# Final stage of a hybrid-mixer and expert layer: residual rows before expert rows, whole adds on VectorE

## The reference

```
h = h + hybrid_mixer(rms_norm(h, mix_norm_w), ...)
xn = rms_norm(h, ffn_norm_w)
h = h + hierarchical_moe(xn, ...)      # two expert rows a token
out = rms_norm(h, final_norm_w)[:, N_META:]
```

## Time and profile before

| | us |
|---|---|
| median of 3 timed runs | 1332.23 |
| lowest, highest | 1330.84, 1334.21 |
| the profiled execution | 1330.3 |
| its span in the trace | 1328.4 |

### The profile page before, as it was taken

How to read it: one execution, slowest core, us unless ns; L and a number is a source line. 1 busy time by engine, 2 the same in 40 slices (tenths; PEclk the granted TensorE clock), 3 DMA queues, 4 the chain that set the end, 5 groups by cost and what they waited for, 6 DMA issues and landing times.

```text
span 1328.4 us, 19059 instructions
## 1 busy us (share of the span) xinstructions
PE 1289.4 (97%) x7544; PEld 1128.8 (85%) x7544; DVE 902.2 (68%) x1060; ACT 722.6 (54%) x919; POOL 178.5 (13%) x144
## 2 busy tenths in 40 slices
PE   6999999999999999999998999999999999999987
PEld 5989999999999999967887788888888888888864
DVE  6654545455545464634247998898898898988867
ACT  6351235123612351423214887888887888888744
POOL 0020112011201120420001011111111111111000
PEclk9999999999999999999996999999999999999999
DMA  7100010001000000306534999999999999999978
GB/s 208 49 16 33 17 33 33 32 18 33 33 19 31 33 33 1 128 7 262 165 145 169 341 387 370 387 380 386 408 393 382 391 386 375 392 384 390 370 276 345
DMA packets 38047, 273.56 MB, mean 206 GB/s; under 512 B 8147, under 2 KB 8403, under 8 KB 25700
## 3 DMA queue, kind: packets, MB, share of 16 engines
q1 hardware_dynamic: 28340, 251.67, 49.9%
q0 software_dynamic: 9216, 16.80, 3.3%
q10 hardware_dynamic: 432, 4.27, 0.8%
HBM read 260.11 MB, written 29.36 MB: 218 GB/s over the span
## 4 chain that ended last, share of the span: by engine, by line
PE 85%; DVE 6%; DMA 4%; ACT 3%; issue 1%; SPq 0%; DVEq 0%; POOLq 0%; ACTq 0%
PE bank L590 11%; PE bank L592 11%; PE bank L591 11%; PE bank L1290 8%; PE bank L1292 8%; PE bank L1291 8%; PE bank L1417 4%; PE bank L1415 3%; DMA w_raw<-in_w_up 3%; PE bank L477 2%; PE bank L481 2%; PE bank L479 2%; PE bank L581 2%; DVE w_lo L955 1%; DVE arena L1820 1%; PE bank L1406 1%
## 5 line engine op out<-in xcount | busy, mean ns | idle before, releaser
L955 DVE TENSOR_TENSOR w_lo<-w_raw,w_hi 128x2048 fp32r<-128x2048 f32 x192 | 432.9, 2286 | 35.2 <-ACT w_hi L736 34.8
L736 ACT ACTIVATE w_hi<-w_raw 128x2048 fp32r<-128x2048 f32 x192 | 360.6, 1915 | 82.3 <-DMA w_raw<-in_w_up 52.4
L1290 PE MATMUL bank<-xn_hi,p_hi 128*128 128x364 f32 (+1 forms) x672 | 229.0, 341 | 2.1 <-DVE p_lo L1755 2.1
L1292 PE MATMUL bank<-xn_hi,p_lo 128*128 128x364 f32 (+1 forms) x672 | 216.5, 322 | 0.0
L1291 PE MATMUL bank<-xn_lo,p_hi 128*128 128x364 f32 (+1 forms) x672 | 216.0, 321 | 0.0
L590 PE MATMUL bank<-w_hi,xgT_hi 128*128 128x512 f32 x512 | 206.3, 403 | 2.9 <-DVE xgT_lo L1013 2.9
L592 PE MATMUL bank<-w_hi,xgT_lo 128*128 128x512 f32 x512 | 201.2, 393 | 0.0
L591 PE MATMUL bank<-w_lo,xgT_hi 128*128 128x512 f32 x512 | 200.7, 392 | 0.0
L1290 PEld LDWEIGHTS bank<-xn_hi,p_hi 128*128 128x128 f32 x672 | 127.5, 190 | 2.9 <-DVE p_lo L1755 2.5
L1291 PEld LDWEIGHTS bank<-xn_lo,p_hi 128*128 128x128 f32 x672 | 127.7, 190 | 0.3
L1292 PEld LDWEIGHTS bank<-xn_hi,p_lo 128*128 128x128 f32 x672 | 127.1, 189 | 0.0
(11 more groups left out here) (253 smaller groups left out, 2032.5 us busy)
## 6 DMA issues: line engine op xcount, KB each, us to landing
w_raw<-in_w_down SPq DMA_DIRECT2D x32, 2048.0 KB, 10.3
w_raw<-in_w_gate SPq DMA_DIRECT2D x31, 2048.0 KB, 10.9
w_raw<-in_w_up SPq DMA_DIRECT2D x31, 2048.0 KB, 9.8
p_raw<-in_w_tiles SPq DMA_DIRECT2D x28, 512.0 KB, 3.3
arena<-y_rows SPq DMA_DIRECT2D x8, 1024.0 KB, 14.2
arena<-in_tokens SPq DMA_DIRECT2D x10, 416.0 KB
w_out_raw<-in_w_out SPq DMA_DIRECT2D x4, 1024.0 KB, 7.9
arena<-in_tokens SPq DMA_DIRECT2D x8, 512.0 KB, 4.3
```

Of the source, the lines that this page charges most:

```text
L736: nc.scalar.activation(w_hi[m][:, half], wraw[m][:, half], ACT.Copy).then_inc(hi_done[m], 1)
L955: nc.vector.tensor_tensor(w_lo[m][:, half], wraw[m][:, half], w_hi[m][:, half].bitcast(F32), ALU.subtract).then_inc(lo_done[m], 1)
L1290: nc.tensor.matmul(out[:, 0:n], p_hi[slot][:, k, :], hi, start=(k == 0), stop=False)
L1292: m = nc.tensor.matmul(out[:, 0:n], p_lo[slot][:, k, :], hi, start=False, stop=(k == KD - 1))
```

## The change

SyncE loads all eight tiles of residual rows before it waits for `moe_done`; before, it loaded tiles 4 to 7 between the expert rows. VectorE adds the whole first expert row (1024 columns) to the residual, where it added 512 columns. TensorE has two identity products a tile in place of three. The order of the functions on each engine stays, and no semaphore or buffer is new.

```diff
-            for t in range(4):
+            for t in range(FT):
                 residual_rows(t)
             sp.wait_ge(moe_done, 1)
             for t in range(FT):
                 if t == 4:
                     sp.wait_ge(u_done, E)
                 sp.dma_start(yf[t].rearrange("p (k d) -> p k d", k=2), ...)
-                if 2 <= t < 6:
-                    residual_rows(t + 2)
...
                 nc.tensor.matmul(pair_of[0], ident, yf[t][:, D:D + 512], start=True, stop=False)
                 nc.tensor.matmul(pair_of[1], ident, yf[t][:, D + 512:2 * D], start=True, stop=False)
-                nc.tensor.matmul(pair_of[1], ident, yf[t][:, 512:D], start=False, stop=False)
...
-            def first_half(t):
+            def first_row(t):
                 dve.wait_ge(hf_loaded[t], 48 if t + NXS < NC else 32)
                 dve.wait_ge(yf_loaded[t], 16)
-                tt(hf[t][:, 0:512], hf[t][:, 0:512], yf[t][:, 0:512], ALU.add).then_inc(f_sum, 1)
+                tt(hf[t], hf[t], yf[t][:, 0:D], ALU.add).then_inc(f_sum, 1)
...
-            first_half(0)
-            first_half(1)
+            first_row(0)
+            first_row(1)
...
-            first_half(2)
+            first_row(2)
             for t in range(FT):
                 from_psum(t)
                 if t:
                     scaled(t - 1)
                 if t + 3 < FT:
-                    first_half(t + 3)
+                    first_row(t + 3)
             scaled(FT - 1)
```

## The result

The changed kernel is slower. Its median is 1336.8 us (10 runs, 1334.81 to 1342.0) against 1331.38 for the kernel before in runs beside it (10 runs, 1329.52 to 1338.02). The ratio is 1.0039, 95% interval 1.0024 to 1.0054, that is 5.2 us (3.2 to 7.2). The forecast of no change that can be measured, +0.9 us at 1333.1 us, was wrong, and the time lies 0.6 us above the range (1330.0 to 1336.2).

The account below looks back on a forecast made before the run. TensorE bounded the last stage at 3.50 us a tile; VectorE would take over at 3.53. A delay of 2.2 us less 1.3 gave +0.9 on the median of 1332.2, so 1333.1 us, range 1330.0 to 1336.2.

Parts of the forecast that it names:

- x: Delay of expert 30's scatter and everything behind GpSimd's memset, put at 2.2 us; the end moves by x - 1.3.
- The extra wait of 4.8 us: Extra hold of an earlier scatter behind weight packets, scaled by packet size to 1.3 us for the last scatter.
- The turn-taking: Scatter and residual packets alternating on the DMA engines once the scatter starts; 1.4 us, of which 0.9 was counted.
- TensorE doesn't hold it up: Last stage: TensorE waits about 1 us for expert 31's low half, then at 2.64 us a tile stays ahead of VectorE.
- the clock as a rival: TensorE pauses before its first last-stage tile and drops to 1.2 GHz: +16 us, 1348; chance 0.02.
- the bound moved from TensorE to VectorE: Last stage: VectorE needs 3.53 us a tile, TensorE 2.64, so the period stays near the earlier 3.50.
- the 6.9 us of TensorE's products: Gain from one identity product fewer a tile, 8 x 0.86 us, if TensorE alone bounded the last stage; chance 0.04.
- The neutral point: Start of VectorE's third whole add at which the change neither gains nor loses: 1298.6, against 1297.11 before.
- the scatter waits for the drained queue: Rival: expert 30's scatter is held until the residual rows are drained, x from 4.2 to 5.4, 1335.7 us; chance 0.18.

Follow-up runs that it names:

- e3: Changed kernel with the two low-half instructions of expert 31 ahead of VectorE's second whole add; ratio to the kernel before 1.0019.
- e1: Changed kernel with residual tiles 4 to 7 loaded between the expert rows again, so only the compute part is new; ratio to the kernel before 1.0005.
- e6: Changed kernel with residual tiles 4 to 7 issued only once the last scatter has landed, still ahead of the expert rows; ratio to the kernel before 1.0014.
- e7: Changed kernel with loads in the old order, low half of expert 31 first, SyncE waiting for the scatters itself; ratio to the kernel before 0.9983.
- e8: As e7, but tiles 5 to 7 go back to half adds and three identity products; ratio to the kernel before 0.9982.
- e9: Kernel before with one edit: SyncE waits for the scatters itself instead of for GpSimd's memset; ratio to the kernel before 0.9993.
- e4: As e1, but 2 MB of unused weights, in packets four times as large, load where the changed kernel loads residual tiles 4 to 7; one run, 1337.87 us.
- e2: Kernel before with only the new load order, keeping half adds and three identity products; ratio to the kernel before 1.0043.
- e5: Changed kernel with only residual tiles 4 and 5 ahead of the memset, tiles 6 and 7 between the expert rows; ratio to the kernel before 1.0009.

## Why the prediction was wrong

The step that failed is the size of x: "The extra wait of 4.8 us, shrunk by 4/14.6, is 1.3 us." I had a row of a scatter held under load, and scaled its hold with the size of the packets, without a row that showed such a law. The runs show that there is none over these ranges: with packets of 4 KB, with packets four times as large, and with 1.88 to 2.95 MB to move, the first packet is at 4.1 to 4.3 us. Against the 1.5 of before that is an extra wait of 2.7, where I had 1.3. The turn-taking behind it was mis-sized too: from the first packet to the landing the scatter took 3.1 us in place of 1.6, 1.5 more, where I counted 0.9. So x is 4.3, not 2.2. That is 2.1 of the 3.6 us by which the trace missed.

The row I scaled was also a poor one to scale: its issue took 2.20 us, that of the last scatter 0.97. The scatter of 1208.26 in the same trace has an issue of 1.07 and a first packet at 4.2, behind weight packets; taken as it is, it would have given the extra wait of 2.7.

The other 1.5 us is a step that I worked out for an undelayed stage and didn't work out again with x: "TensorE doesn't hold it up". Behind the late memset the second whole add waits until 1298.85, the low half of expert 31 is queued behind it on VectorE, and TensorE waits 4.63 us where I wrote about 1. The second rows also came 3.87 us after the first and not 2.57. Then came the lower clock and a second tile of 4.0 us. e3 moves the two instructions and takes 1.6 us away. I had the clock as a rival for the whole stage, at +16 us; it was low for one tile.

Right, by the same steps: the bound moved from TensorE to VectorE (3.53 us a tile forecast and measured, whole adds 1.22 to 1.23 long and stepping by 1.13), so the 6.9 us of TensorE's products were worth nothing by themselves (e1). The neutral point held too. It was put at 17.96 us after the scatter's issue (1298.6 - 1280.64) for the third add; the measured 20.69, with the 0.2 that the fourth add waits and the 1.47, gives 4.4 for the measured 4.45.

The rival "the scatter waits for the drained queue" named the place and, with x from 4.2 to 5.4 and 1335.7 us, nearly the time. That it came near is luck, since its reason is not what happened: the scatter started with 2.4 us of loads still to come. I gave it 0.18 since the packets are 3.6 times smaller. All loaded scatters in the earlier trace rows spoke for it, with a median of 11.8 us against 3.1, and one mechanism of my own making spoke against it.

## What to carry to other kernels

A load that is moved ahead of a wait fills a gap in the transfers, but ask whose transfer used that gap. Here it was the scatter that everything behind the wait depends on; 2 MB saved from the busy stretch cost 4.3 us at its start. When a transfer's delay under load has to be guessed, look through the loaded rows for one like it in all else, its issue time above all, and take that delay as it is; a scaling law needs rows of its own. And once a start is late, go through each engine's queue again: the instruction that waits for it blocks what stands behind it, here two short instructions that TensorE needed.

## What the runs showed that was not expected

- A scatter issued by GpSimd while SyncE's queue has much to move (1.88 to 2.95 MB) moved its first packet 4.1 to 4.3 us after its issue in six kernels, with 4 KB packets and with 16 KB packets, and 1.5 us after it where the queue had 0.07 to 0.58 MB to move (before, e6, e7, e8, e9). What makes up the 4.2 us is open: a fixed amount of bytes ahead (some 1.3 MB, 0.41 MB/us in the 3.2 us that follow the 0.97 of the issue; 1.4 MB in e4) and a fixed time, each cut short when the queue runs dry, fit these runs about equally well. A fixed number of packets doesn't.
- TensorE's clock during expert 31's last product was not the same from kernel to kernel, though the idle time ahead of it was. It was low in part of it in the changed kernel, e1, e2, e5 and e7, and not in the seven other traces. The changed kernel shows it low from 1288 on, the kernel before does not, in the same stretches (first the changed kernel, then before):

```profile
1288.00:1290.00 2.00, 2.00 (x8) 1.55 (x7) 1.66 (x1) 0.00 (x0) 0.09 (x1) 0.63 0.02 8
1290.00:1292.00 2.00, 2.00 (x7) 1.55 (x6) 0.00 (x0) 0.00 (x0) 0.00 (x0) 0.52 0.40 88
...
1288.00:1290.00 2.00, 2.00 (x10) 1.67 (x9) 1.56 (x1) 0.00 (x0) 0.00 (x0) 1.00 1.01 393
1290.00:1292.00 2.00, 2.00 (x10) 1.65 (x10) 0.69 (x1) 0.00 (x0) 0.00 (x0) 1.00 1.02 416
```

  It made the product 1.5 to 1.6 us longer in the changed kernel, e1 and e7. In the changed kernel this was hidden behind the second rows (until 1298.85), in e1 behind the third (whose add waits 0.71 for them); in e7 it was not. What decides whether the clock falls here no run shows.
